# Seven half products for ten of the eleven pairs of SwiGLU tiles, with the residual kept in DRAM meanwhile

## The reference, cut to what matters

```python
def _swiglu(x, w_gate, w_up, w_down):
    hid = jax.nn.silu(jnp.einsum('bsd,df->bsf', x, w_gate)) * jnp.einsum('bsd,df->bsf', x, w_up)
    return jnp.einsum('bsf,fd->bsd', hid, w_down)
...
for l in range(DEPTH):
    h = h + 0.5 * _swiglu(_rmsnorm(h, ffn1_norm[l]), ffn1_w_gate[l], ffn1_w_up[l], ffn1_w_down[l])
    h = h + _hybrid_mixer(_rmsnorm(h, mix_norm[l]), w_in[l], ...)
    h = h + 0.5 * _swiglu(_rmsnorm(h, ffn2_norm[l]), ffn2_w_gate[l], ffn2_w_up[l], ffn2_w_down[l])
```

## Time and profile before

| | us |
|---|---|
| median of 3 runs | 3229.08 (3227.15 to 3229.86) |
| profiled execution, its own time | 3232.4 |
| its span, first to last instruction | 3230.5 |
| PE busy in it | 3167.1 |
| DVE busy | 2025.7 |
| ACT busy | 1457.1 |
| HBM read | 291.03 MB, 91 GB/s |

### The profile page before, as it was taken

How to read it: one execution, slowest core, us unless ns; L and a number is a source line. 1 busy time by engine, 2 the same in 40 slices (tenths; PEclk the granted TensorE clock), 3 DMA queues, 4 the chain that set the end, 5 groups by cost and what they waited for, 6 DMA issues and landing times.

```text
span 3230.5 us, 43458 instructions
## 1 busy us (share of the span) xinstructions
PE 3167.1 (98%) x17020; PEld 2697.5 (83%) x17020; DVE 2025.7 (63%) x3095; ACT 1457.1 (45%) x2145; POOL 71.0 (2%) x137
## 2 busy tenths in 40 slices
PE   9999999999999999999999999999999999999998
PEld 7988876788988899887678898888888888889987
DVE  7853565767843686346575785467766687468633
ACT  5542335454532454233545553346445476345422
POOL 0000000100000000000010000000000000000000
PEclk9999999999999999999999999999999999999999
DMA  4333322122333233332211233332322223323331
GB/s 142 105 110 95 97 82 75 34 69 85 102 113 99 87 98 117 95 97 88 69 46 43 92 105 115 97 104 92 105 92 82 87 91 102 106 85 99 118 91 66
DMA packets 102746, 296.80 MB, mean 92 GB/s; under 512 B 15440, under 2 KB 26464, under 8 KB 102544
## 3 DMA queue, kind: packets, MB, share of 16 engines
q1 hardware_dynamic: 96336, 277.91, 27.2%
q0 software_dynamic: 5344, 14.02, 1.6%
q10 hardware_dynamic: 864, 2.10, 0.2%
HBM read 291.03 MB, written 2.95 MB: 91 GB/s over the span
## 4 chain that ended last, share of the span: by engine, by line
PE 85%; DVE 7%; ACT 5%; issue 2%; DMA 1%; POOL 0%; DVEq 0%; ACTq 0%; POOLq 0%
PE ps L928 26%; PE ps L930 26%; PE ps L929 26%; PE ps L937 2%; ACT wh L1579 1%; DVE wl L2226 1%; DVE mf L2539 1%; ACT L1559 1%; PE ps L942 1%; PE ps L1460 1%; PE ps L1307 1%; PE ps L1340 1%; PE ps L1456 0%; PE ps L1390 0%; ACT mf L2140 0%
## 5 line engine op out<-in xcount | busy, mean ns | idle before, releaser
L1579 ACT ACTIVATE wh<-raw 128x1024 fp32r<-128x1024 f32 (+3 forms) x634 | 621.9, 982 | 1105.6 <-PE ps L930 1063.2
L2226 DVE TENSOR_TENSOR wl<-raw,wh 128x1024 fp32r<-128x1024 f32 (+3 forms) x634 | 716.0, 1129 | 512.2 <-ACT wh L1579 508.8
L928 PE MATMUL ps<-hnh,wh 128*128 128x512 f32 (+1 forms) x2492 | 918.8, 369 | 6.9 <-DVE hnl L2345 3.3
L929 PE MATMUL ps<-hnl,wh 128*128 128x512 f32 (+1 forms) x2492 | 904.5, 363 | 0.0
L930 PE MATMUL ps<-hnh,wl 128*128 128x512 f32 (+1 forms) x2492 | 904.3, 363 | 0.0
L928 PE MATMUL ps<-mr,wh 128*128 128x512 f32 (+1 forms) x2180 | 758.4, 348 | 0.9 <-DVE mr L2844 0.5
L930 PE MATMUL ps<-mr,wl 128*128 128x512 f32 (+1 forms) x2180 | 755.3, 346 | 0.0
L929 PE MATMUL ps<-mr,wh 128*128 128x512 f32 (+1 forms) x2180 | 754.9, 346 | 0.0
L928 PEld LDWEIGHTS ps<-hnh,wh 128*128 128x128 f32 x2492 | 473.7, 190 | 86.4 <-issue 11.4
L930 PEld LDWEIGHTS ps<-hnh,wl 128*128 128x128 f32 x2492 | 473.2, 190 | 74.0
L929 PEld LDWEIGHTS ps<-hnl,wh 128*128 128x128 f32 x2492 | 473.9, 190 | 71.8 <-issue 2.7
(11 more groups left out here) (343 smaller groups left out, 2826.4 us busy)
## 6 DMA issues: line engine op xcount, KB each, us to landing
raw<-in_w_in SPq DMA_DIRECT2D x140, 512.0 KB, 3.4
raw<-in_ffn_w_gate SPq DMA_DIRECT2D x87, 512.0 KB, 3.5
raw<-in_ffn_w_up SPq DMA_DIRECT2D x87, 512.0 KB, 4.2
raw<-in_ffn_w_down SPq DMA_DIRECT2D x64, 512.0 KB, 3.5
raw<-in_w_ffn_in SPq DMA_DIRECT2D x44, 512.0 KB, 3.5
raw<-in_ffn_w_down SPq DMA_DIRECT2D x32, 384.0 KB, 3.1
raw<-in_w_out SPq DMA_DIRECT2D x32, 256.0 KB, 2.7
mf<-cs_rows POOLq DMA_DIRECT2D x32, 256.0 KB, 3.8
```

The lines of the kernel that those rows point to most:

```text
L928: self.e.matmul(out, ah, bh, start=start, stop=False, skip_group_check=shared)
L929: self.e.matmul(out, ah, bl, start=False, stop=False, skip_group_check=shared)
L1579: self.e.activation(k.spl[k.spl_of[u]][0][:, 0:n], x[:, 0:n], ACT.Copy).then_inc(k.w_hi, 1)
L2226: self.e.tensor_tensor(lo[:, 0:n], x[:, 0:n], hi[:, 0:n].bitcast(F), ALU.subtract).then_inc(k.w_lo, 1)
```

## The change

- `SEVEN` now holds pairs 1 to 10, each with gate and up: 20 seven-products in each FFN, 100 in all. Pair 0 alone is plain. The compiled program has 1620 more matmuls on PE.
- ACT first multiplies halves of h with the gain, 16 activations of 128x256 (`x1`, then `x2`), and DVE then works on 128x1024 (`t1`, `t3`, `t2`, `t4`), in place of its operations on 128x256. All steps stand beside pair 0, at a pace of 1.0.
- The high and low parts of two of the sums (for E3 and B2) now lie where h was. So GpSimd stores h to DRAM after `x1` (`swap_h`, one DMA of 128x4096, 2.1 MB), ACT waits for `h_out` before it writes there, and GpSimd loads h back after the last seven-product's `c1`. The first `add_h` of an FFN waits for `h_back`.
- The fourth sum is written over the second token halves of `hn` 0 to 3, as a tenth step after A1 of the first seven-product.

```diff
-F_T, F_D, F_X, F_3, F_2, F_4, F_PACE = (28, 32, 36, 40), 12, 14, 16, 18, 20, 0.6
+F_1, F_D, F_X, F_3, F_2, F_4, F_PACE = 40, 12, 14, 16, 18, 20, 1.0
-SEVEN = {p: (up,) for p, up in ((2, True), (3, True), (4, False), (5, True), (6, True), (7, True))}
+SEVEN = {p: (True,) for p in range(1, 11)}
...
             if n == A1:
                 self.end_pair()
+                if i == 2 * min(SEVEN) and not hid:
+                    self.halves_step(f, 9)
...
# Scalar.halves_step
+        if n in (0, 1):
+            self.wait_ge(k.h_set, 8)
+            for x, half, first in (((F_2, 0, 0), (F_X, 256, 0)), ((F_3, 256, 4), (F_4, 0, 4)))[n]:
+                for j in range(4):
+                    m = e.activation(k.slot(x, 2)[:, 256 * j:256 * j + 256], k.h[first + j][:, half:half + 256], ACT.Copy,
+                                     scale=k.cl(gain, g + first + j))
+            m.then_inc(*k.ft_a.up(f, f"x{n + 1}"))
...
+        elif n in (6, 7):
+            name, at, x, scale = (("3", 1, F_3, 1.0), ("2", 2, F_2, -1.0))[n - 6]
+            self.wait_ge(*k.ft_v.at(f, "t3" if n == 6 else "t2"))
+            self.wait_ge(*k.ft_a.at(f, "x2"))
+            self.wait_ge(k.h_out, 16 * (f + 1))
...
# Vector.halves_step
+        if n == 2:
+            self.wait_ge(*k.ft_a.at(f, "x1"))
+            e.tensor_tensor(d[:, :], t2[:, :], x[:, :], ALU.subtract).then_inc(*k.ft_v.up(f, "t1"))
         elif n == 3:
+            self.wait_ge(*k.ft_a.at(f, "x2"))
+            e.tensor_tensor(t3[:, :], t3[:, :], x[:, :], ALU.subtract).then_inc(*k.ft_v.up(f, "t3"))
...
# Vector.add_h
             g = k.tmp(0)
+            self.wait_ge(k.h_back, 16 * (f + 1))
...
+def swap_h(k, e, f):
+
+    e.wait_ge(*k.ft_a.at(f, "x1"))
+    e.dma_start(k.h_save, k.h_all[:, :]).then_inc(k.h_out, 16)
+    e.wait_ge(*k.se_v.at(2 * len(SEVEN) * (f + 1) - 1, "c1"))
+    e.wait_ge(k.h_out, 16 * (f + 1))
+    e.dma_start(k.h_all[:, :], k.h_save).then_inc(k.h_back, 16)
```

More of the change, by code:

```diff
@@ L244, in place @@
             return t
-        self.h = [place(f"h{i}", T) for i in range(8)]
+        self.h_base = self.at
+        self.h_all = place("h", 8 * T)
+        self.h = [self.h_all[:, T * i:T * i + T] for i in range(8)]
+        self.h_sums = [nc.alloc_sbuf_tensor_at(f"hs{i}", [128, 1024], R, offset=self.h_base + 4096 * i) for i in range(4)]
+        self.h_save = nc.dram_tensor("h_save", (128, 8 * T), F).ap()
+        self.h_out, self.h_back = sem("h_out"), sem("h_back")
         self.hn_base = self.at
@@ L293, in turned, with moving @@
     def turned(self, n):
-        return self.slot(F_T[n], 2, R), self.slot(F_T[n] + 2, 2, R)
+        return (self.slot(F_1, 2, R), self.slot(F_1 + 2, 2, R)) if n == 0 else self.h_sums[2 * n - 2:2 * n]
+    def moving(self, n, j):
+        if n == 3:
+            return [x[:, 256:512] for x in self.hn[j]]
+        return [x[:, 256 * j:256 * j + 256] for x in self.turned(n)]
     def part(self, i, h):
@@ L1044, in half_product @@
             else:
-                hi, lo = k.turned(moving)
-                s = slice(256 * j, 256 * j + 256)
+                hi, lo = k.moving(moving, j)
+                s = slice(0, 256)
             up = None
@@ L1620, in halves_step @@
         gain, g = F_GAIN[f]
-        if n == 1:
-            self.wait_ge(*k.ft_v.at(f, "d"))
-            for j in range(4):
[L1624 to L1630, removed]
+        if n in (0, 1):
[5 more added lines that the diff above has]
+            m.then_inc(*k.ft_a.up(f, f"x{n + 1}"))
+        elif n == 3:
+            self.wait_ge(*k.ft_v.at(f, "t1"))
+            e.activation(k.turned(0)[0][:, :], k.slot(F_D, 2)[:, :], ACT.Copy).then_inc(*k.ft_a.up(f, "h1"))
+        elif n in (6, 7):
[3 more added lines that the diff above has]
+            self.wait_ge(k.h_out, 16 * (f + 1))
+            e.activation(k.turned(at)[0][:, :], k.slot(x, 2)[:, :], ACT.Copy, scale=scale).then_inc(*k.ft_a.up(f, "h" + name))
+        elif n == 9:
+            self.wait_ge(k.unit_done, self.u)
+            self.wait_ge(*k.ft_v.at(f, "t4"))
+            for j in range(4):
+                m = e.activation(k.moving(3, j)[0], k.slot(F_4, 2)[:, 256 * j:256 * j + 256], ACT.Copy, scale=-1.0)
+            m.then_inc(*k.ft_a.up(f, "h4"))
     def ffn_silu(self, f, i):
@@ L2285, in halves_step @@
         k, e = self.k, self.e
-        gain, g = F_GAIN[f]
-        one, two = slice(0, 256), slice(256, 512)
         at = [slice(256 * j, 256 * j + 256) for j in range(4)]
         d, x, t3, t2, t4 = (k.slot(i, 2) for i in (F_D, F_X, F_3, F_2, F_4))
[L2290 to L2305, removed]
+        if n == 2:
+            self.wait_ge(*k.ft_a.at(f, "x1"))
+            e.tensor_tensor(d[:, :], t2[:, :], x[:, :], ALU.subtract).then_inc(*k.ft_v.up(f, "t1"))
@@ L2306, in halves_step @@
         elif n == 3:
+            self.wait_ge(*k.ft_a.at(f, "x2"))
+            e.tensor_tensor(t3[:, :], t3[:, :], x[:, :], ALU.subtract).then_inc(*k.ft_v.up(f, "t3"))
+        elif n == 4:
             self.wait_ge(*k.ft_v.at(f, "t3"))
[L2308 to L2318, removed]
+            e.tensor_tensor(t2[:, :], t2[:, :], t3[:, :], ALU.add).then_inc(*k.ft_v.up(f, "t2"))
@@ L2319, in halves_step @@
         elif n == 5:
             self.wait_ge(*k.ft_v.at(f, "t2"))
[L2321 to L2326, removed]
+            e.tensor_tensor(t4[:, :], t4[:, :], t2[:, :], ALU.subtract).then_inc(*k.ft_v.up(f, "t4"))
@@ L2327, in halves_step @@
+            hi, lo = k.turned(0)
+            self.wait_ge(*k.ft_a.at(f, "h1"))
+            e.tensor_tensor(lo[:, :], d[:, :], hi[:, :].bitcast(F), ALU.subtract).then_inc(*k.ft_v.up(f, "l1"))
+        elif n in (7, 8):
+            name, to, t, scale = (("3", 1, t3, 1.0), ("2", 2, t2, -1.0))[n - 7]
             hi, lo = k.turned(to)
@@ L2330, in halves_step @@
                                    op0=ALU.mult, op1=ALU.subtract).then_inc(*k.ft_v.up(f, "l" + name))
+        elif n == 9:
+            self.wait_ge(*k.ft_a.at(f, "h4"))
+            for j in range(4):
+                hi, lo = k.moving(3, j)
+                m = e.scalar_tensor_tensor(out=lo, in0=t4[:, at[j]], scalar=-1.0, in1=hi.bitcast(F),
+                                           op0=ALU.mult, op1=ALU.subtract)
+            m.then_inc(*k.ft_v.up(f, "l4"))
     def multiply_tokens(self, banks, half, j):
@@ L3151, in pool_program @@
     for l in range(2):
+        swap_h(k, e, 2 * l)
         e.wait_ge(k.unit_done, k.marks["small"][l])
@@ L3188, in pool_program @@
         k.set_blocks(e, l, 1, D_X, k.blk_x)
+        swap_h(k, e, 2 * l + 1)
     e.wait_ge(*k.sr_v.at(0, "cs"))
```

3 lines of the change are left out of this document (2 added, 1 removed).

## The result

The changed kernel takes 3234.74 us (median of 20 runs, 3231.29 to 3239.72), the kernel before on the same chip 3228.92 (20 runs, 3225.74 to 3232.47). The ratio is 1.0018, 95% interval 1.0011 to 1.0025: slower, by 5.8 us, where 12.3 were forecast. The profiled execution took 3231.78 us, one of the shortest of the 20, and that of before 3232.4, one of its longest.

The account below looks back on a forecast made before the run. The prediction took PE, busy 3167.1 of 3230.5 us, as the bound. Losses of 13.8 (FFN 0), 28.0 (FFNs 1 to 4) and 6.5 (ends) against 36.0 won gave 12.3 us slower, 3241.4 us, range 3231 to 3256.

Parts of the forecast that it names:

- seven-products in place of plain: All FFNs: 45 more seven-products, each 0.80 us less than two tiles by plain products; 36.0 us less if nothing waits.
- FFN 0: pause, net: FFN 0, before the banks open: PE idle 11.7 us until up 1 is read, 10.8 more than before.
- FFN 0: clock behind it: FFN 0, after the pause: clock at half speed for some 6 us of work, costing 3.0 us.
- FFNs 1 to 4: Start of each later FFN: waits before the fourth product, A1 and B2, plus clock; 7.0 us each, 28 in all.
- five ends: End of each FFN's seven-products: PE waits for the last bank's read before the down products; 1.3 us each, 6.5 in all.
- the rest of the program: Everything outside the FFNs: the forecast sum holds no term for it.
- B2's wait: FFNs 1 to 4, first seven-products: B2 needs `l2` and ACT's copy of A1's bank; 1.1 us lost in each.
- a store well under 8 us: Store of h to DRAM, put at 9.0 us within 8.0 to 12.4; a much shorter one was a sign of error.
- (c): Rival, FFNs 1 to 4: reads of up 0 and gate 1 do not hold PE up; faster, down to 3213; chance 0.07.
- (a): Rival, all FFNs: clock stays up and the DMA takes 8 us; about 40 lost, 3233, no measurable change; chance 0.17.
- (b): Rival, all FFNs: slow store and low clock in every FFN; 63 us lost, 3256; chance 0.13.
- (d): Rival, long run of seven-products: it drags, 0.2 us in each of 100, 20 more, 3261; chance 0.05.

Follow-up runs that it names:

- E3: Not a run: a product on PE within a seven-product, after A1 and before B2, that reads the high and low parts of a sum of token halves.
- early_end: Changed kernel with only pairs 1 to 7 by seven-products, pairs 8 to 10 plain; 3250.15 us, ratio 1.0067 to the kernel before.
- two_stores: Changed kernel with GpSimd storing h twice in a row before it reports h as out; 3256.65 us, ratio 1.0089 to the kernel before.
- pace75: Changed kernel with `F_PACE` 0.75 in place of 1.0, spreading the steps over one product more; 3230.95 us, ratio 1.0003 to the kernel before.
- a_again: Changed kernel run once more, unchanged, for a second profile; span 3236.3 us, one run.
- late_up0: Changed kernel with seven-products from pair 2, pace 0.6, and in FFNs 1 to 4 sums begun after tile 0's up product; 3203.59 us, ratio 0.9921.
- late_end: late_up0 with PE waiting for `c1` behind the first down product, not ahead of it; 3197.10 us, ratio 0.9902 to the kernel before.

## Why the prediction was right, and where its sizes were off

| step | predicted | in the trace of after |
|---|---|---|
| seven-products in place of plain | -36.0 | -36.0 (10.08 each throughout) |
| FFN 0: pause, net | 10.8 | 23.14 - (34.62 - 4 x 5.44) = 10.3 |
| FFN 0: clock behind it | 3.0 | 203.42 - 201.95 = 1.5, less 0.1 before |
| FFNs 1 to 4 | 28.0 | 26.8 |
| five ends | 6.5 | 5 x 1.3 = 6.5 |
| sum over the FFNs | +12.3 | +9.0 (by whole FFNs +8.9) |
| the rest of the program | 0 | -3.1 by the medians |

The mechanism was the one forecast: the saving comes in full, and waits of PE at the start and end of each FFN eat more than all of it. Three sizes were off, the clock, B2's wait and the unchanged stages.

**The saving** came in full. early_end shows that it does so at the end of the row too.

**FFN 0.** The pause was forecast at 11.7 us and measured at 11.18, with the right releaser. That is partly luck. One of the prediction's own signs of being wrong came true, a store well under 8 us: it was put at 9.0 us with bounds of 8.0 and 12.4, and took 6.6. The Trainium skill, DMA: Bandwidth & Descriptors, "Anatomy of one DMA — SWDGE (gpsimd) path", gave 6.8, and the trace agrees.

The bounds failed because the nearest rows were small transfers and stores that other engines issued, and I took the traffic of weights on top, though the weight buffers were full. The 322 GB/s of the earlier trace rows is the mean of a window in which the DMA engines were busy for 0.82, so a running store is faster (322 / 0.82 = 393, an estimate); and no run shows the start-up of 1.5 us that was added.

But the store was not the last condition: behind it DVE's queue (lines 2505, 2251, 2321, 2324, 2327) ended 1.8 us later. My path for DVE stopped too early. From `t3` to the start of `l3` it is 6.6 us in the trace (40.92 to 47.48), and from the 42.8 of the forecast that gives 49.4, where the store of 9.0 us gave 49.65: nearly the same read of up 1, without the store. It follows that the 12.8 us for a fast store and the 2.2 us less for one of 6.8 were wrong too; a store below some 8.7 us gains nothing here. two_stores shows both: of 8.3 us more of store all but 1.8 turn into pause.

**The clock.** The sign was right and the size was not. After FFN 0's pause, 3.0 was forecast from the earlier trace rows, for 6 us of work at half speed, and 1.4 measured: the clock had fallen by 44 us, within the pause, and was low for only some 3 us of the work behind it. In each later FFN, 0.6 was forecast; there the clock fell too, and seven-products took 4.4 to 4.6 us more than the 201.95, of which A1's wait is some 3.0 (3.16 to 3.20 from start to start, less the 0.12 between two such matmuls without a wait). The other 1.4 to 1.6 is the low clock, and the window from 755 gives nearly the same: 0.34 of 5 us is 1.7, a little of it ahead of A1.

**FFNs 1 to 4.** The fourth product was put at R+10.5 and started at R+10.39 (747.08); A1 was put at R+19.5 and started at R+19.51 (756.20). The gate before them is read behind a chain of 19 us, as rival (c) says, but its "count of queued operations" is not all work: 4.7 us of it DVE waits for ACT. B2's wait of 1.1 us doesn't appear in the first profile of after. It does in pace75, 1.11 us idle in FFN 1, and in FFNs 2 and 3 of a_again, 0.87 idle (1.15 from start to start). There the low clock fell on the fourth product, A1's wait shrank to 1.44 and 1.32, and the clock was up at B2; where A1 and E3 run at the low clock, PE arrives later and the wait is hidden. So the step on B2 and the step on the clock were not two terms to be added but two that replace each other: 3.1 + 1.1 + 0.6 = 4.8 forecast, 4.4 to 4.6 measured. With the fourth product at 2.5 to 2.6 and before's own short wait (0.75 in two FFNs) each loses 6.2 to 7.2; 7.0 was forecast.

**The ends** were right at 1.3 us by the stage, though the idle time shown is only 1.01: from start to start it is 1.29 us in late_up0 for 0.12 in late_end, and the first matmul behind the wait shows 0.50 us for 0.40. late_end shows the cause by taking the wait away. The load of h back took 9.7 us and no wait for it shows.

**The rest of the program** was put at nothing. Its code is unchanged, but its time, by the medians, is 3.1 us less. That is the step by which 9 became 5.8; the mixers' clock is where it shows, and what moves the clock stays open.

**The rivals.** (a) came nearest in time (3233), for another reason than it named: the clock did not stay up. Its 8 us for the DMA were still too long, and that changed little. (b) fell with the store's 6.6 us. (c) needed less than 3.9 us in each later FFN and got 6.2 to 7.2. (d) fell by the windows of 10.08 and by early_end. The chance of 0.20 for a result within 0.2%, where the median came out, was too small: the steps inside the FFNs came out 3.3 us lower and the unchanged stages 3.1, either of them half of what was needed, and the forecast lay only 5.9 us above the bound of 3235.5.
